# Gates and hidden values of the V product loaded in halves of four experts instead of quarters of two

## The chip, the cores and the metric

The kernel runs on one core of a Trainium2 chip. The metric is the device time in microseconds of one execution; lower is better. The text calls TensorE PE, VectorE DVE, ScalarE ACT, GpSimd POOL and SyncE SP, as the profile does.

## The reference

One layer of a streaming encoder: an input projection, a convolution mixer and a gated linear attention, an output projection, a layer norm, and then a mixer called PEER. The change lies in the last product of PEER. It is this part, cut to what matters:

```python
ids, gates = top 16 of 128 x 128 product keys for each of 8 heads of a token
h = gelu(einsum('td,thkd->thk', xb, u_table[ids]))
w = gates * h
out = einsum('thk,thkd->td', w, v_table[ids])
x = layer_norm(ALPHA * x + out)
```

There are 544 tokens (512 of the prompt, 32 of the sample), 16,384 experts, and rows of 2,048 float32 in u_table and v_table. A token picks 128 experts.

## The kernel before

**Two ways to the same sum.** For 352 tokens (TD) the last product is done densely: a gate matrix g, zero except at the picks, is multiplied by h, and PE multiplies all of V by w = g * h. For the other tokens the picked rows of V are gathered from DRAM by POOL and added on DVE, a slot of 128 rows at a time (192 slots in all; one gather brings 128 rows of 8 KB, 1 MB). Both run at the same time in the stage here called V.

**Stage V.** V is streamed in 128 tiles of 1 MB, in 16 groups of 8 tiles. For each tile:

- SP loads it into `wraw[:, m % 2]` (`v_tile_in`). It may do so once DVE has split the tile that held this half two tiles ago.
- ACT rounds it to float32r in `wh` (L1133), and DVE forms the rest `wl = wraw - wh` (`v_lo_split`, L2040).
- PE runs 48 matmuls of 352 columns: wh with Wh (L1060), wh with Wl (L1061), and last wl with Wh (L1066).
- DVE adds PE's two sums to `acc` (`add_pair`, L2015; L2034 for a single one).

`Wh` and `Wl` hold w of a whole group of 8 x 128 experts, and each exists twice. While PE is in group g, DVE and ACT make those of group g + 1: for each pair q of the 8 expert columns DVE multiplies `wt = hg * gt` (`w_products`, L1993), ACT rounds it to `Wh` (L1475), and DVE forms `Wl` (`w_lows`, L1999). `gt` and `hg` are single buffers of 8 x 352 per partition. `gt` is read from the scratch tensor g_scratch, `hg` from h_scratch, both in DRAM.

**The order on DVE is written out by hand**, as a loop over tiles n = 8g + m. I call such a turn step m of group g. The products of the next group stand in steps 3, 4, 5 and 6, the lows in steps 4, 5, 6 and once more in step 6 behind the first slot. The part of a step that all have is:

```python
add_pair(n)
todo = list(slots_at(n))
for s in todo[:1]:
    slot(s)
...
v_lo_split(n + 2)
for s in todo[1:]:
    slot(s)
```

`slots_at` gives a step one or two slots, 1.66 on average. Steps 0 and 1 have almost nothing to add: three of the 16 output blocks are kept in PSUM to the end (`KEEP`), so step 0 adds nothing and step 1 one block.

**The gathers** have three buffers `gath`. POOL issues `v_gather(s)` when slot s - 3 is done (it waits for `slot_s`), and behind each of them an `h_gather` of 128 single values for a slot eight further on. slot s on DVE waits for its gather.

**The order on SP**: SP issues the tile of its turn (g, m) when DVE has done the split in its step 8g + m - 4, so SP's turn m = 4 follows DVE's step 0, and SP's turn m = 0 follows step 4 of the group before. Behind a tile stands a load for the next group. All of them go through one DMA queue (q1); POOL's gathers go through another (q0). `used(g, q)` makes SP wait until the products that read the old contents are done.

Of the kernel before, what the change touches and what calls it, by code (L numbers as in the profile page):

```python
# [48 lines left out]
EG = 8  # L49
NG = NKEY // EG  # L50
GC = 32
RT, NB = 64, 2
TD = T - P - RT
# [17 lines left out]
def n_op(kind, i):  # L71

    if kind == 4:
        return 7 * i + 8 if i + 1 < NP else 7 * i + 6
    if i == 0:
        return (1, 2, 5, 6, 3, 7).index(kind)
    return 7 * i - 1 + (1, 2, 4, 5, 6, 3, 7).index(kind)
# [75 lines left out]
def program(nc, xT, w_in, w_f, w_out, w_q, u_t, v_t, conv_state, conv_w, conv_vec, gla_state,  # L153
# [3 lines left out]
    with ctx:  # L157
        lo0 = -(-nc.sbuf_base // 32) * 32

        def at(name, shape, dt, off):  # L160
            return nc.alloc_sbuf_tensor_at(name, shape, dt, offset=lo0 + off)

        def sem(name):
            return ctx.enter_context(nc.semaphore(name))
# [72 lines left out]
        o = M1  # L237
# [22 lines left out]
        o = 15520 + 5 * XB + RT * 4  # L260
# [24 lines left out]
        gt = at("gt", [P, EG, TD], F32, S0)  # L285
        hg = at("hg", [P, EG, TD], F32, HG)
# [53 lines left out]
        zero_set, g_zero, g_ids, g_put, pk_s = (  # L340
            sem("zeros_set"), sem("g_cleared"), sem("g_indices"), sem("g_scattered"), sem("rest_packed"))
        h_st = [sem("h_stored0"), sem("h_stored1")]
        g_in = [sem(f"g_pair{q}_in") for q in range(EG // 2)]
        h_in = [sem(f"h_pair{q}_in") for q in range(EG // 2)]

        h_out, w_s, y_add = sem("gelu_out"), sem("w_pair_ready"), sem("y_added")
        xt_s, xt_hi, xt_lo = sem("x_sum"), sem("x_sum_hi"), sem("x_sum_lo")
# [5 lines left out]
        wp_s, wh_s = sem("w_pair_product"), sem("w_pair_hi")  # L353
# [25 lines left out]
        h_dense = h_flat[NKEY * P * SD:].rearrange("(g p n u t) -> g n p u t", g=NG, p=P, u=2, t=TD)  # L379
        h_group = h_flat[NKEY * P * SD:].rearrange("(g p q) -> g p q", g=NG, p=P)  # L380
# [74 lines left out]
        def _(sp):  # L455
            def load(dst, src, s):
                sp.dma_start(dst, src).then_inc(s, 16)
# [62 lines left out]
            for t in range(2 * NP):  # L520
# [7 lines left out]
                g, m = (KU + t) // EG, (KU + t) % EG  # L528
# [1 line left out]
                v_rows_in(g, m)  # L530
            vs = v_t.rearrange("(g n) p k c -> g n p k c", n=EG)

            def g_pair(g, q):
                a = g_rows[g] if isinstance(g, int) else g_rows[bass.ds(g, 1)].rearrange("o j e t -> (o j) e t")
                load(gt[:, 2 * q:2 * q + 2], a[:, 2 * q:2 * q + 2], g_in[q])

            def h_pair(g, q):
                a = h_dense[g, q] if isinstance(g, int) else h_dense[bass.ds(g, 1), q].rearrange("o p u t -> (o p) u t")
                load(hg[:, 2 * q:2 * q + 2], a, h_in[q])

            def v_tile_in(g, m):
                sp.wait_ge(dlo, g * EG + (A_V + m - 1 - D0))
                tile(vs[g, m] if isinstance(g, int) else vs[bass.ds(g, 1), m].rearrange("o p k c -> (o p) k c"), m % 2)

            def used(g, q):
                sp.wait_ge(wp_s, g * (EG // 2) + (q + 1))

            sp.wait_ge(op_lo, n_op(4, NP - 2) + 1)
            tile(vs[0, 0], 0)
            sp.wait_ge(g_put, 16 * PUTS * PH)  # L550
            for q in range(EG // 2):
                g_pair(0, q)
            for v in range(2):
                sp.wait_ge(h_st[v], 32 * (EG // 4))
            sp.wait_ge(prod, n_op(5, NP - 1) + 1)
            for q in range(EG // 2):
                h_pair(0, q)

            def acc_load(j):
                load(acc[:, 4 * j:4 * j + 4], x2_dram[:, 4 * j:4 * j + 4], acc_in[j])  # L560
# [10 lines left out]
            for m in range(2, EG):  # L571
                v_tile_in(0, m)
                if m == 2:
                    for v in range(2):
                        sp.wait_ge(h_st[v], 32 * (NKEY // 4))
                if m < 6:
                    used(0, m - 2)
                    g_pair(1, m - 2)
                    h_pair(1, m - 2)
                else:  # L580
                    used(1, m - 6)
                    g_pair(2, m - 6)

            def v_group_in(g, last=False):

                for m in range(EG):
                    v_tile_in(g, m)
                    if m < 2:
                        used(g, m + 2)
                        g_pair(g + 1, m + 2)  # L590
                    elif m < 6:
                        h_pair(g + 1, m - 2)
                    elif not last:
                        used(g + 1, m - 6)
                        g_pair(g + 2, m - 6)

            with sp.Fori(1, NG - 2) as g:
                v_group_in(g)
            v_group_in(NG - 2, True)
            for m in range(EG):  # L600
                v_tile_in(NG - 1, m)
            for k in range(0, KT, 2):
# [917 lines left out]
        def _(v_):  # L1520
# [28 lines left out]
            def gla(h):  # L1549
# [16 lines left out]
                def distances(l):  # L1566

                    b, n, m = blocks(bcum, l)
                    d, _, _ = blocks(dist[l % 2], l)
                    mid = b[:, :, 0, m - 1:m].to_broadcast([P, n, m])  # L1570
                    tt_(d[:, :, 0], mid, b[:, :, 0], ALU.subtract)
                    C.done(tt_(d[:, :, 1], b[:, :, 1], mid, ALU.subtract), dist_s)
# [410 lines left out]
            def v_lo_first(n):  # L1983
                v_.wait_ge(whi, A_V + n + 1)
                C.inc(tt_(wl[:, n], wraw[:, n], f(wh[:, n]), ALU.subtract), dlo)

            def w_products(g, q):

                e = slice(2 * q, 2 * q + 2)
                v_.wait_ge(g_in[q], g * 16 + 16)  # L1990
                v_.wait_ge(h_in[q], g * 16 + 16)
                v_.wait_ge(w_s, g * (EG // 2) + q)
                C.inc(tt_(wt[:], hg[:, e], gt[:, e], ALU.mult), wp_s)  # L1993

# [66 lines left out]
            def w_lo(e):  # L2061
                v_.wait_ge(wh0_s, e + 1)
                C.inc(tt_(Wl[0][:, e], wt[:, e % 2], f(Wh[0][:, e]), ALU.subtract), w0_s)

            for e in range(EG):
                if e % 2 == 0:
                    v_.wait_ge(g_in[e // 2], 16)
                    v_.wait_ge(h_in[e // 2], 16)
                if e >= 2:
                    v_.wait_ge(w0_s, e - 1)  # L2070
                C.inc(tt_(wt[:, e % 2], hg[:, e], gt[:, e], ALU.mult), wp0_s)
                if e == 1:
                    v_lo_first(0)
                if e:
                    w_lo(e - 1)
# [16 lines left out]
            for n in range((NG - 1) * EG):  # L2092
                g, m = n // EG, n % EG
                if n == (NG - 2) * EG:
                    v_.wait_ge(slot_s, SLOTS)
                    v_.sem_inc(y_sp_s, 1)
                if n > (NG - 2) * EG and m <= 4:
                    v_.wait_ge(y_turn, m)
                    a_ = acc[:, 4 * m - 4:4 * m, T - P:T]
                    C.inc(stt_(a_, a_, ALPHA, ps[:, TURN].rearrange("p (k t) -> p k t", k=4), ALU.mult, ALU.add),  # L2100
                          y_sp_u)
                if 4 <= m < 7:
                    w_lows(g + 1, (g + 1) % 2, m - 4)
                if 3 <= m < 7:
                    w_products(g + 1, m - 3)
# [4 lines that stand above are left out]
                if m == 6:  # L2110
                    w_lows(g + 1, (g + 1) % 2, 3)
# [3 lines that stand above are left out]
# [112 lines left out]
```

## Time and profile before

| | |
|---|---|
| three runs | 3569.99, 3570.5, 3574.88 us |
| median | 3570.5 us |
| the profiled execution's own time | 3572.87 us |
| its span, first to last instruction | 3571.1 us |
| mean granted TensorE clock in it | 0.986 |
| PE, DVE, POOL, ACT busy over the span | 96%, 78%, 55%, 33% |
| DMA moved over the span | 815.58 MB |

The time is that of the whole program; stage V is about its last 1,060 us. The shares of busy time are means over stages with different limits, so the shares above say little of V; the rows below are of V, most of them of the 861 us from 2542.5 to 3403.7, in which 13 whole groups run alike. The profiled execution is 2.4 us above the median.

### The profile page before, as it was taken

Reading aid. Unit: us, or ns where it says so; the run is one execution under the profiler, and the core shown is the slowest. Engines: PE = TensorE matmul, PEld = TensorE weight load, DVE = VectorE, ACT = ScalarE, POOL = GpSimd, SP = SyncE. Lnnn points to the kernel's source line nnn. Section 1 sums busy time; section 2 is a strip of 40 time slices with the busy share of each in tenths; the row PEclk is TensorE's granted clock in tenths of the full one; section 3 lists DMA queues with packets and bytes.
Section 4 is the critical chain, followed back from the end, with each engine's and each line's share of the span. In section 5 each row is a group of like instructions: output and inputs, shape, how many; then the busy total and the mean of one; then the engine's idle time right before and its main releaser. Section 6 shows DMA issues by size and latency. Waiting matters only on the chain. (4 is left out here: it accounts for less than half of the span.)

```text
span 3571.1 us, 62917 instructions
## 1 busy us (share of the span) xinstructions
PE 3442.1 (96%) x25376; PEld 3393.3 (95%) x25376; DVE 2790.6 (78%) x3529; ACT 1187.1 (33%) x1155; POOL 1960.7 (55%) x1165
## 2 busy tenths in 40 slices
PE   8999999998999999999999999999999999999996
PEld 7999999898999999999999999999989999999996
DVE  4866858624799887777777777777898999999997
ACT  2332333323222234444444444443322222222323
POOL 3443434445444577778768850000777778788741
PEclk9999999899999999999999999999999999999998
DMA  4222222473225678888888887777999999999982
GB/s 154 75 77 78 82 73 72 171 285 122 82 91 172 186 207 228 225 228 218 230 224 227 224 224 226 227 228 260 388 369 379 390 366 390 383 374 392 382 320 108
DMA packets 467598, 815.58 MB, mean 228 GB/s; under 512 B 76128, under 2 KB 373632, under 8 KB 399632
## 3 DMA queue, kind: packets, MB, share of 16 engines
q1 hardware_dynamic: 337920, 543.80, 46.3%
q0 software_dynamic: 85184, 201.75, 16.8%
q10 hardware_dynamic: 44368, 68.47, 5.2%
q8 instruction: 64, 1.05, 0.1%
q14 instruction: 62, 0.51, 0.0%
HBM read 740.81 MB, written 207.22 MB: 265 GB/s over the span
## 5 line engine op out<-in xcount | busy, mean ns | idle before, releaser
L618 POOL TENSOR_TENSOR wl<-wraw,wh 128x512 fp32r<-128x512 f32 x352 | 538.6, 1560 | 689.6 <-ACT wh L1133 681.7
L669 POOL DMA_INDIRECT g_scratch<-picks,g_col x384 | 635.7, 1655 | 185.0 <-issue 152.5
L1060 PE MATMUL ps<-Wh,wh 128*128 128x352 f32 x2032 | 660.6, 327 | 49.6 <-DVE Wl L1999 44.6
L1133 ACT ACTIVATE wh<-wraw 128x2048 fp32r<-128x2048 f32 x216 | 413.6, 1915 | 865.0 <-DMA wraw<-in_v_t 478.4
L1061 PE MATMUL ps<-Wl,wh 128*128 128x352 f32 x2032 | 658.1, 326 | 0.0
L1008 PE MATMUL ps<-xh,wl 128*128 128x272 f32 x1792 | 518.8, 290 | 0.0
L1008 PE MATMUL ps<-xl,wh 128*128 128x272 f32 x1792 | 516.0, 288 | 0.0
L1008 PE MATMUL ps<-xh,wh 128*128 128x272 f32 x1792 | 515.8, 288 | 0.3 <-DVE wl L1925 0.3
L710 PE MATMUL ps<-xh,wh 128*128 128x272 f32 x2304 | 491.0, 294 | 17.5 <-DVE ext L1683 11.9
L710 PE MATMUL ps<-xl,wh 128*128 128x272 f32 x2304 | 482.4, 291 | 0.0
L655 POOL DMA_INDIRECT s_h<-h_scratch,s_hid x128 | 245.4, 1917 | 422.2 <-DMA h_scratch<-hb 383.5
L1414 ACT ACTIVATE wh<-wraw 128x1024 fp32r<-128x1024 f32 x280 | 297.1, 1062 | 498.4 <-PE ps L1008 367.4
L1060 PEld LDWEIGHTS ps<-Wh,wh 128*128 128x128 f32 x2032 | 387.1, 191 | 55.5 <-issue 50.6
L710 PEld LDWEIGHTS ps<-xh,wh 128*128 128x128 f32 x2304 | 364.8, 191 | 28.9 <-issue 24.8
L1061 PEld LDWEIGHTS ps<-Wl,wh 128*128 128x128 f32 x2032 | 388.9, 191 | 0.0
L1925 DVE TENSOR_TENSOR wl<-wraw,wh 128x1024 fp32r<-128x1024 f32 x280 | 343.1, 1226 | 47.9 <-ACT wh L1414 39.6
L710 PEld LDWEIGHTS ps<-xl,wh 128*128 128x128 f32 x2304 | 365.2, 190 | 0.0
L1066 PE MATMUL ps<-Wh,wl 128*128 128x352 f32 x2032 | 346.8, 323 | 0.0
L1008 PEld LDWEIGHTS ps<-xh,wh 128*128 128x128 f32 x1792 | 337.6, 188 | 0.5 <-DVE wl L1925 0.5
L1008 PEld LDWEIGHTS ps<-xl,wh 128*128 128x128 f32 x1792 | 337.9, 189 | 0.0
L1008 PEld LDWEIGHTS ps<-xh,wl 128*128 128x128 f32 x1792 | 337.4, 188 | 0.0
L2058 DVE SCALAR_TENSOR_TENSOR y_sp<-gath,s_w,y_sp 128x2048 f32<-128x2048 f32 x127 | 298.5, 2350 | 47.9 <-DMA gath<-v_rows,s_ids 31.9
(319 smaller groups left out, 7039.5 us busy)
## 6 DMA issues: line engine op xcount, KB each, us to landing
wraw<-in_u_t SPq DMA_DIRECT2D x128, 1024.0 KB, 5.2
v_rows<-in_v_t SPq DMA_DIRECT2D x256, 512.0 KB
wraw<-in_v_t SPq DMA_DIRECT2D x128, 1024.0 KB, 8.1
wraw<-in_w_in SPq DMA_DIRECT2D x40, 1024.0 KB, 4.8
g_scratch<-zeros ACTq DMA_DIRECT2D x32, 704.0 KB, 6.4
h_scratch<-hb ACTq DMA_DIRECT2D x64, 352.0 KB, 8.2
gt<-g_scratch SPq DMA_DIRECT2D x64, 352.0 KB, 7.7
hg<-h_scratch SPq DMA_DIRECT2D x64, 352.0 KB, 10.4
```

Of the source, the lines that this page charges most:

```text
L618: ins = nc.gpsimd.tensor_tensor(wl[:, u, part], wraw[:, u, part], f(wh[:, u, part]), ALU.subtract)
L655: nc.gpsimd.indirect_dma_start(column(s_h, x_h, s), None, h_elem, bass.IndirectOffsetOnAxis(ap=column(s_hid, x_hid, s), axis=0)).then_inc( ...
L669: nc.gpsimd.indirect_dma_start(g_elem, bass.IndirectOffsetOnAxis(ap=idx, axis=0), gate, None, compute_op=ALU.add).then_inc(g_put, 16)
L710: ins = mat(out[:, h], w[:, u, k], m[:, k, halves[h]], start=(begin and k == ks[0] and w is wh and m is ah), stop=(end and k == ks[-1] and ...
L1008: ins = mat(bank(kind), w[:, k], m[:, k], start=(k == 0 and w is ah and m is bh), stop=(k == HK - 1 and w is al))
L1060: mat(out, wh[:, u, d * EG + e], Wh[v][:, e], start=(begin and e == 0), stop=False)
L1061: mat(out, wh[:, u, d * EG + e], Wl[v][:, e], start=False, stop=False)
L1066: ins = mat(out, wl[:, u, d * EG + e], Wh[v][:, e], start=False, stop=(end and e == EG - 1))
L1133: go(wh[:, u], wraw[:, u], ACT.Copy).then_inc(whi, 1)
L1414: go(op_part(wh, q), op_src(kind, i), ACT.Copy).then_inc(op_hi, 1)
L1925: C.inc(tt_(op_part(wl, q), op_src(kind, i), f(op_part(wh, q)), ALU.subtract), op_lo)
L2058: C.inc(stt_(y[:], gath[s % 3][:], w, y[:], ALU.mult, ALU.add), slot_s)
```

## The change

The pieces are twice as large and half as many. Before, SP loads a pair of expert columns at a time, 352 KB, one behind each tile: the gates of group g + 1 in SP's turns 6 and 7 of the group before and in turns 0 and 1, and the hidden values in turns 2, 3, 4 and 5. After, it loads four columns at a time, 704 KB: gates behind the tiles of turns 0 and 3, hidden values behind those of turns 2 and 5, and nothing behind those of turns 1, 4, 6 and 7. There are two semaphores for the gates and two for the hidden values where there were four each, and DVE's products wait for the half that holds their pair.

```diff
-            def g_pair(g, q):
+            def g_half(g, j):
+                e = slice(4 * j, 4 * j + 4)
                 a = g_rows[g] if isinstance(g, int) else g_rows[bass.ds(g, 1)].rearrange("o j e t -> (o j) e t")
-                load(gt[:, 2 * q:2 * q + 2], a[:, 2 * q:2 * q + 2], g_in[q])
-
-            def h_pair(g, q):
-                a = h_dense[g, q] if isinstance(g, int) else h_dense[bass.ds(g, 1), q].rearrange("o p u t -> (o p) u t")
-                load(hg[:, 2 * q:2 * q + 2], a, h_in[q])
+                load(gt[:, e], a[:, e], g_in[j])
+
+            def h_half(g, j):
+                e = slice(4 * j, 4 * j + 4)
+                a = h_group[g] if isinstance(g, int) else h_group[bass.ds(g, 1)].rearrange("o p q -> (o p) q")
+                load(hg[:, e], a[:, 4 * j * TD:4 * (j + 1) * TD].rearrange("p (e t) -> p e t", e=4), h_in[j])
...
-            def used(g, q):
-                sp.wait_ge(wp_s, g * (EG // 2) + (q + 1))
+            def used(g, j):
+                sp.wait_ge(wp_s, g * (EG // 2) + 2 * (j + 1))
...
-                if m < 6:
-                    used(0, m - 2)
-                    g_pair(1, m - 2)
-                    h_pair(1, m - 2)
-                else:
-                    used(1, m - 6)
-                    g_pair(2, m - 6)
-
-            def v_group_in(g, last=False):
+                if m in (2, 4):
+                    used(0, m // 2 - 1)
+                    g_half(1, m // 2 - 1)
+                elif m in (3, 5):
+                    h_half(1, m // 2 - 1)
+
+            def v_group_in(g):
 
                 for m in range(EG):
                     v_tile_in(g, m)
-                    if m < 2:
-                        used(g, m + 2)
-                        g_pair(g + 1, m + 2)
-                    elif m < 6:
-                        h_pair(g + 1, m - 2)
-                    elif not last:
-                        used(g + 1, m - 6)
-                        g_pair(g + 2, m - 6)
-
-            with sp.Fori(1, NG - 2) as g:
+                    if m in (0, 3):
+                        used(g, m // 3)
+                        g_half(g + 1, m // 3)
+                    elif m in (2, 5):
+                        h_half(g + 1, m // 3)
+
+            with sp.Fori(1, NG - 1) as g:
                 v_group_in(g)
-            v_group_in(NG - 2, True)
...
-                v_.wait_ge(g_in[q], g * 16 + 16)
-                v_.wait_ge(h_in[q], g * 16 + 16)
+                v_.wait_ge(g_in[q // 2], g * 16 + 16)
+                v_.wait_ge(h_in[q // 2], g * 16 + 16)
```

On SP's queue, the loop over groups begins with the tile of turn 0. `wraw<-in_v_t` is a tile, `gt` the gates, `hg` the hidden values; ISA and REGISTER_ALU rows are SP's waits and address arithmetic. Before:

```order
-L457 DMA wraw<-in_v_t 128x2048
-L546 ISA
-L457 ISA
-L457 DMA gt<-g_scratch 128x704
-L457 ISA
-L457 DMA wraw<-in_v_t 128x2048
-L546 REGISTER_ALU
-L457 ISA
-L457 DMA gt<-g_scratch 128x704
```

And after, at the same place, turns 0, 1 and 2:

```order
+L457 DMA wraw<-in_v_t 128x2048
+L548 ISA
+L457 ISA
+L457 DMA gt<-g_scratch 128x1408
+L457 ISA
+L457 DMA wraw<-in_v_t 128x2048
+L544 REGISTER_ALU
+L457 ISA
+L457 DMA wraw<-in_v_t 128x2048
+L457 ISA
+L457 DMA hg<-h_scratch 128x1408
```

The two pairs behind two tiles have become one half behind the first of them; the first half of the hidden values stands where the first pair of them stood.

Further on in the same loop, SP's turns 3, 4 and 5, which follow DVE's steps 7, 0 and 1. Before:

```order
-L457 DMA wraw<-in_v_t 128x2048
-L457 ISA
-L457 DMA hg<-h_scratch 128x704
-L542 REGISTER_ALU
-L457 ISA
-L457 DMA wraw<-in_v_t 128x2048
-L457 ISA
-L457 DMA hg<-h_scratch 128x704
-L542 REGISTER_ALU
-L457 ISA
-L457 DMA wraw<-in_v_t 128x2048
```

And after:

```order
+L457 DMA wraw<-in_v_t 128x2048
+L548 REGISTER_ALU
+L457 ISA
+L457 DMA gt<-g_scratch 128x1408
+L544 REGISTER_ALU
+L457 ISA
+L457 DMA wraw<-in_v_t 128x2048
+L544 REGISTER_ALU
+L457 ISA
+L457 DMA wraw<-in_v_t 128x2048
+L457 ISA
+L457 DMA hg<-h_scratch 128x1408
```

Behind the tile of turn 3 a half of the gates has moved in, which was spread over later turns before; turn 4 carries nothing, and turn 5 a half.

## Rows read from the trace of the kernel before

**Rows 1.** The page: span, and DMA share in 40 slices

```profile
span 3571.1 us, 62917 instructions
DMA  4222222473225678888888887777999999999982
```

**Rows 2.** What PE waited for, 2542.5 to 3403.7: total us, times, longest

```profile
PE ps L1060 <- DVE Wl L1999: 39.2, 12, 5.3
```

**Rows 3.** What DVE waited for, 2542.5 to 3403.7

```profile
DVE y_sp L2058 <- DMA gath<-v_rows,s_ids: 31.9, 28, 4.1
DVE y_x L2058 <- DMA gath<-v_rows,x_ids: 12.7, 13, 1.8
DVE acc L2015 <- PE ps L1066: 0.6, 1, 0.6
```

**Rows 4.** Windows, from the last low of a group to the next first product

```profile
core 0: us, PE busy (x) PEld busy (x) DVE busy (x) ACT busy (x) POOL busy (x), PEclk, DMA share, GB/s
2676.90:2711.20 34.30, 34.14 (x212) 34.14 (x213) 29.35 (x17) 6.76 (x4) 27.78 (x15) 1.00 0.95 378
...
3140.10:3172.80 32.70, 32.55 (x194) 32.56 (x195) 28.30 (x17) 7.66 (x4) 26.51 (x15) 0.95 0.99 397
...
sum 442.80, PE 441.04 PEld 441.15 DVE 389.82 ACT 100.67 POOL 356.37; mean PE 33.93 PEld 33.93 DVE 29.99 ACT 7.74 POOL 27.41
```

**Rows 5.** Windows, from the first product to the last low of a group

```profile
2643.90:2676.90 33.00, 30.13 (x188) 29.84 (x186) 30.59 (x23) 12.64 (x9) 23.15 (x13) 1.00 0.94 363
...
3303.10:3335.00 31.90, 29.44 (x184) 29.15 (x183) 30.68 (x24) 10.70 (x8) 22.27 (x13) 1.00 0.98 384
...
sum 418.40, PE 372.24 PEld 366.98 DVE 398.51 ACT 137.88 POOL 315.89; mean PE 28.63 PEld 28.23 DVE 30.65 ACT 10.61 POOL 24.30
```

**Rows 6.** SP's queue in order of time, group 5

```profile
2811.24 0.33 SPq L457 DMA_DIRECT2D wraw<-in_v_t  x1
2811.75 0.33 SPq L457 DMA_DIRECT2D hg<-h_scratch  x1
...
2841.34 0.33 SPq L457 DMA_DIRECT2D wraw<-in_v_t  x1
2845.05 0.33 SPq L457 DMA_DIRECT2D gt<-g_scratch  x1
```

**Rows 7.** DVE in order of time, group 5

```profile
2829.63 2.29 DVE L2040 TENSOR_TENSOR wl<-wraw,wh 128x2048 fp32r<-128x2048 f32 x1
...
2836.62 2.35 DVE L2058 SCALAR_TENSOR_TENSOR y_sp<-gath,s_w,y_sp 128x2048 f32<-128x2048 f32 x1 [1.33 <-DMA gath<-v_rows,s_ids]
2838.89 2.29 DVE L2040 TENSOR_TENSOR wl<-wraw,wh 128x2048 fp32r<-128x2048 f32 x1
```

**Rows 8.** ACT in order of time, group 5

```profile
2826.29 1.92 ACT L1133 ACTIVATE wh<-wraw 128x2048 fp32r<-128x2048 f32 x1 [6.01 <-DMA wraw<-in_v_t]
2834.86 1.92 ACT L1133 ACTIVATE wh<-wraw 128x2048 fp32r<-128x2048 f32 x1 [6.65 <-DMA wraw<-in_v_t]
```

**Rows 9.** DMA issues, 2542.5 to 3403.7: count, KB each, median us to landing

```profile
wraw<-in_v_t SPq DMA_DIRECT2D x104, 1024.0 KB, 8.4
hg<-h_scratch SPq DMA_DIRECT2D x52, 352.0 KB, 10.5
gt<-g_scratch SPq DMA_DIRECT2D x52, 352.0 KB, 7.7
```

**Rows 10.** Windows, us 2461 (the first pairs of gates alone) and 8.2 us of group 9

```profile
2461.00:2462.00 1.00, 1.00 (x11) 1.00 (x10) 1.00 (x2) 0.53 (x1) 0.00 (x0) 1.00 1.02 406
3096.60:3104.80 8.20, 8.20 (x53) 8.20 (x53) 5.43 (x4) 3.31 (x2) 5.63 (x5) 1.00 1.02 419
```

**Rows 11.** POOL in order of time, group 5

```profile
2830.84 1.90 POOL L650 DMA_INDIRECT gath<-v_rows,s_ids  x1 [0.30 <-issue]
2833.03 1.96 POOL L655 DMA_INDIRECT s_h<-h_scratch,s_hid  x1 [0.30 <-issue]
2835.30 0.94 POOL L650 DMA_INDIRECT gath<-v_rows,s_ids  x1 [0.30 <-issue]
```

More of the change, by code:

```diff
@@ L342, in program @@
         h_st = [sem("h_stored0"), sem("h_stored1")]
-        g_in = [sem(f"g_pair{q}_in") for q in range(EG // 2)]
-        h_in = [sem(f"h_pair{q}_in") for q in range(EG // 2)]
+        g_in = [sem(f"g_half{j}_in") for j in range(2)]
+        h_in = [sem(f"h_half{j}_in") for j in range(2)]
         h_out, w_s, y_add = sem("gelu_out"), sem("w_pair_ready"), sem("y_added")
@@ L550, in _ @@
             sp.wait_ge(g_put, 16 * PUTS * PH)
-            for q in range(EG // 2):
-                g_pair(0, q)
+            for j in range(2):
+                g_half(0, j)
             for v in range(2):
@@ L555, in _ @@
             sp.wait_ge(prod, n_op(5, NP - 1) + 1)
-            for q in range(EG // 2):
-                h_pair(0, q)
+            for j in range(2):
+                h_half(0, j)
             def acc_load(j):
@@ L2065, in _ @@
             for e in range(EG):
-                if e % 2 == 0:
-                    v_.wait_ge(g_in[e // 2], 16)
-                    v_.wait_ge(h_in[e // 2], 16)
+                if e % 4 == 0:
+                    v_.wait_ge(g_in[e // 4], 16)
+                    v_.wait_ge(h_in[e // 4], 16)
                 if e >= 2:
```

## The prediction

> **What bounds the kernel now.** I read the page first. The share of the DMA engines stands at 9 tenths only in the last quarter of the span [rows 1], and that quarter is stage V, the only place that the change touches. So all that follows is read in V, and there in the 861 us in which 13 groups run alike (66.2 us each).
>
> Next come the waits of PE, since PE has the most work in the program. In V it waits at one place: for DVE's last `Wl` of a group, 39.2 us in 12 times [rows 2]. So PE is held up once a group, for about 3.3 us, and by DVE. Then DVE's own waits: for PE 0.6 us in all, for gathers 31.9 + 12.7 = 44.6 us in 41 times [rows 3]. DVE is therefore the chain that sets V: it never waits for PE, PE waits for it, and what it loses itself it loses to gathers that have not landed. In this stretch a microsecond more or less of DVE's waiting is a microsecond of the kernel.
>
> Where in a group does DVE wait? I cut each group in two, at the last low of a group (step 6) and at the next first product (step 3). The first part, which I call the light stretch, lasts 442.8 / 13 = 34.06 us, and DVE works 29.99 of it [rows 4]: 4.07 us idle. The other part, the heavy stretch with the products and lows of the next group, lasts 418.4 / 13 = 32.18 us with 30.65 us of work [rows 5]: 1.53 us idle, most of that the short gaps at semaphores. So nearly all waiting for gathers is in the light stretch, where DVE has little but slots and splits and asks for them quickly.
>
> The same windows show the DMA engines near full in both: 378 to 397 GB/s in the light ones shown [rows 4], middle about 388; 363 to 384 in the heavy ones [rows 5], middle about 373. The light stretch is where requests come faster than the engines can serve them; in the heavy one there is about 15 GB/s, or 4%, to spare.
>
> **The change, part by part.**
>
> *Fewer instructions on SP.* 64 issues of 0.33 us go [rows 6]. SP waits between tiles anyway: from the issue at 2811.75 to its next gates at 2845.05 it is ahead of its work [rows 6]. Price 0. The waits `used` also go away in effect: the products of both pairs of a half are done before SP's turn comes. That lets the gates start earlier behind their tile (before, the gates at 2845.05 left 3.7 us after their tile at 2841.34 [rows 6]), but nothing stood behind that wait that was ready to go, since the next tile waits for DVE's next split, which comes later than the product. Price 0.
>
> *Lateness of the halves.* The pair landed 7.7 (gates) and 10.5 us (hidden values) after issue [rows 9]; a half carries 352 KB more, 0.36 MB / 388 GB/s = 0.93 us, perhaps twice that when it shares the engines. Its least lead is that of the second hidden half, issued after step 1 and used in step 5, that is, more than three steps of some 8 us. No product waits. In the first group the products run right after older work and the pieces are all issued long before; price 0 to 1 us once, and I take 0.
>
> *Larger pieces as such.* Per group 8 pairs of 0.36 MB are moved, 2.88 MB. When only pairs were in flight they ran at 406 GB/s; the best 8 us with large tiles and gathers gave 419 [rows 10]. If the halves reached that, a group saves 2.88/406 - 2.88/419, or 7.1 - 6.9 = 0.2 us of engine time. Bounds: 0, and 0.6 us if each piece also costs a gap at its start that halving saves. I take 0.2, for 14 groups 3 us, as far as it reaches DVE at all.
>
> *Where the bytes go.* This is the term that decides. SP's turns 2, 3, 4 and 5 come after DVE's steps 6, 7, 0 and 1, so what they issue runs in the light stretch. Before, four pairs stand there, 1.44 MB. After, halves stand behind turns 2, 3 and 5: 2.16 MB. The heavy stretch had four pairs and keeps one half. So 0.72 MB per group move from the stretch with DMA time to spare into the one in which DVE waits for DMA. At 388 GB/s they take 1.86 us. Upper bound: all of it is waited for, 1.86 us per group. Nothing comes back in the heavy stretch, because there DVE's own 30.65 us of work are the length. Lower bound: 0, if the last half, behind turn 5, is in fact still running when the heavy stretch begins and the one in turn 3 is made up for by the empty turn 4. The half behind turn 5 is one of the two that moved in or grew, so I take half of the sum, 0.93 us, less a good 0.1 us of the saving: 0.8 us per group. There are 14 light stretches with the new order (at the start of groups 1 to 14): 14 x 0.8 = 11 us.
>
> *Who shares with whom.* A gather that is under way beside a pair gets the larger part of an engine if the engine takes turns piece by piece: rows of 8 KB against 2.75 KB. Against rows of 5.5 KB it gets less. By bytes the four pieces of 2.75 KB and two of 5.5 KB cost the same; so this adds nothing to the sum over a group, but it points the same way in the light stretch. The Trainium skill ("DMA: Bandwidth & Descriptors", Queues, rings and completion order) says that each DMA engine goes round-robin between the queues that have work, switching at packet boundaries. By that rule a gather beside a half is later than one beside a pair, which speaks against the change; by the byte count alone it would not be. No row here shows the turns themselves.
>
> *Tiles.* A tile issued behind a larger piece lands later, by up to 0.36 MB / 388 = 0.93 us, or 1.86 us when a gather takes every second turn. ACT waits for tiles all the time (6.01 and 6.65 us), and finished at 2828.21 and 2836.78 [rows 8] for splits that DVE began at 2829.63 and 2838.89 [rows 7]: slack of 1.4 and 2.1 us. At the lower lateness this costs nothing; at the upper one 1.86 - 1.4 = 0.4 us per group, 6 us in all. It is in the upper end, not in the sum.
>
> The profiled execution took 3572.87 us, 2.4 above the median of 3570.5. The sum, 3572.9 + 11 = 3584, is therefore 3570.5 + 11 = 3581.5 in medians.
>
> **The rivals.**
>
> *It cancels out (no change).* Three light-stretch pieces and an empty turn may be smoothed by the buffers: three gathers and two tiles. For it: in the light stretch POOL issues without a break, gather, small gather, gather at 2830.84, 2833.03 and 2835.30 [rows 11], 4.46 us per slot, while DVE's late slot began at 2836.62, 3.9 us after the gather of 2830.84 had been issued [rows 7, 11]. If the pace of POOL is what DVE feels, more bytes beside it matter little. Against it: 3.9 us for 1 MB is 270 GB/s, so the landing is shared and not free. The time: 0 to 0.5 us per group, 3564 to 3577, middle 3571.
>
> *Faster.* Four of eight turns carry nothing now, and gathers of steps 0 and 1 may find the engines free at just the right time: turn 4, after step 0, carries nothing, and the slots of step 1 and 2 are gathered then. If each light stretch loses 1 us of its 4.07 us idle, 14 us go: 3556. It decides for this side once the empty turn takes off more than the halves at turns 2, 3 and 5 add, that is, if the empty turn is worth more than 1.86 us. The end of it is all of the gather waits, 44.6 us in 13 groups. For it speaks that the waits fall on steps 0 to 2, on both sides of turn 4; against it, that turn 4 loses 0.36 MB and its neighbours gain 0.36 MB each. The Trainium skill (the same page, Rules for kernel authors) asks for at least 1 MiB per DMA and for small transfers to be joined, and gives about 2 us as the fixed part of one; by that, four loads fewer a group would be up to 8 us of engine time, an estimate from that page. The 406 GB/s of pairs that run one behind the other [rows 10] do not show such a gap, so in this kernel the fixed part overlaps.
>
> *Slower than forecast.* All 1.86 us are waited for and the tiles come late as well: 14 x (1.86 + 0.4) = 32 us, 3602.
>
> **How the numbers follow.** A difference under 0.2% (7 us) cannot be told from none here: the three runs lie 5 us apart. Forecast, slower by 7 to 27 us (3578 to 3597): 0.45. Beyond it: 0.05. Cancels: 0.28. Faster: 0.22. So faster 0.22, same 0.28, slower 0.50. The forecast's own range is 3578 to 3597. For 8 in 10 I go down to 3558, which leaves about half of the faster case out, and up to 3599.
>
> **What the profile after would show.** DVE's waits for gathers in the like stretch at 55 to 60 us where they were 44.6; PE's waits for `Wl` at some 50; the light stretches 0.8 us longer, the heavy ones as they were; in the light ones the same GB/s, in the heavy ones less. DVE's busy time, PE's, and the bytes the same. No product waits for `gt` or `hg`. It would be wrong if the light stretches keep their length with more bytes in them (their GB/s up to 405 or so: then the engines had room there), if a DVE split waits for ACT (tiles late), or if gathers land sooner beside fewer, larger pieces.

## The result, and the profile after

The kernel became slower, by 0.45%: ratio 1.0045, 95% interval 1.0033 to 1.0057, median 3589.74 us of five runs where before has 3571.66 us of five. The forecast was 11 us; it is 18 us by medians, 16 us by the ratio.

The profiled execution of the changed kernel took 3588.32 us. Its page, to be held against [rows 1]:

```profile
span 3586.5 us, 62756 instructions
DMA  4222222463225678889888887778999999999982
DMA packets 458382, 815.58 MB, mean 227 GB/s; under 512 B 75104, under 2 KB 372608, under 8 KB 390416
```

The bytes are the same to the last digit shown (815.58 MB). The span is 15.4 us longer.

The waits of PE and DVE, in the 13 like groups (2544.5 to 3417.6 us; lines 4 lower than before), answer to [rows 2, 3]. `DVEq` is DVE's sequencer, and `issue` is time in which the engine waited for nothing that the trace shows. First PE:

```profile
PE ps L1056 <- DVE Wl L1995: 42.9, 12, 5.2
PE ps L1056 <- DVEq L2012: 4.9, 4, 1.7
PE ps L1056 <- issue: 2.1, 1, 2.1
```

And DVE:

```profile
DVE y_sp L2054 <- DMA gath<-v_rows,s_ids: 41.7, 34, 3.9
DVE y_x L2054 <- DMA gath<-v_rows,x_ids: 15.3, 14, 2.9
...
DVE wl L2036 <- ACT wh L1129: 1.4, 1, 1.4
```

DVE waits 41.7 + 15.3 = 57.0 us for gathers where it waited 44.6 us [rows 3], and in 48 places where there were 41. No product waits for `gt` or `hg`; no such row is among the waits. One split waits for ACT, 1.4 us in all. PE's three rows make 49.9 us where the same rows made 43.2 us. For the row of `Wl` some 50 us had been expected, and it is 42.9. PE's busy time did not stay the same either: its 4,992 matmuls took 820.0 us where they took 813.3, at a mean granted clock of 0.983 over the program where it was 0.986. DVE waits for PE nowhere in these groups, so this is not what lengthened them.

The light stretches (last low of a group to the next first product), two of the 13 and the sum, to be held against [rows 4]:

```profile
3283.10:3317.30 34.20, 34.03 (x203) 34.04 (x204) 29.42 (x17) 8.40 (x5) 24.03 (x15) 0.95 0.99 392
3349.20:3385.40 36.20, 36.06 (x225) 36.07 (x226) 31.79 (x19) 9.60 (x5) 28.34 (x16) 1.00 0.98 388
sum 454.60, PE 452.89 PEld 453.00 DVE 390.45 ACT 115.81 POOL 351.56; mean PE 34.84 PEld 34.85 DVE 30.04 ACT 8.91 POOL 27.04
```

And the heavy ones, against [rows 5]:

```profile
3317.30:3349.20 31.90, 29.15 (x183) 28.82 (x181) 30.67 (x24) 9.88 (x8) 22.27 (x13) 1.00 0.96 372
3385.40:3417.60 32.20, 25.92 (x161) 25.34 (x159) 30.62 (x24) 8.93 (x7) 26.03 (x13) 0.98 0.92 358
sum 418.50, PE 367.06 PEld 360.92 DVE 398.19 ACT 123.96 POOL 315.14; mean PE 28.24 PEld 27.76 DVE 30.63 ACT 9.54 POOL 24.24
```

The light stretch grew from 442.8 / 13 = 34.06 to 454.6 / 13 = 34.97 us, with the same work in it (390.45 us where there were 389.82). The heavy ones stayed to a tenth of a microsecond in sum: 418.5 and 418.4. So 11.8 of the 15.4 us lie in 13 light stretches. The rest lies at the ends. The first like group starts at 2544.5 where it was 2542.5 (+2.0), and 1.0 us of that lies ahead of stage V, which the change does not touch:

```profile
2455.63 0.33 SPq L457 DMA_DIRECT2D wraw<-in_v_t  x1
2456.64 0.33 SPq L457 DMA_DIRECT2D wraw<-in_v_t  x1
```

This is the first tile of V, before and after. The stretch of group 14 behind the 13, from the last low to the next, took 71.6 us where it took 68.9 (+2.7). Its light part, which is the 14th light stretch, took 37.8 us where it took 36.5 (+1.3). What follows took 1.3 us less.

### The profile page after: what moved, and what is told of

Same layout as the page of the kernel before. It is cut to its first block and busy times, and to the rows that moved or that the text cites. A ratio compares the mean times of both kernels' runs of the same rounds, so it can differ in the third digit from the quotient of the medians.

```text
span 3586.5 us, 62756 instructions
## 1 busy us (share of the span) xinstructions
PE 3448.6 (96%) x25376; PEld 3399.6 (95%) x25376; DVE 2791.4 (78%) x3529; ACT 1188.5 (33%) x1155; POOL 1956.6 (55%) x1165
## 2 busy tenths in 40 slices
DMA packets 458382, 815.58 MB, mean 227 GB/s; under 512 B 75104, under 2 KB 372608, under 8 KB 390416
## 3 DMA queue, kind: packets, MB, share of 16 engines
q0 software_dynamic: 85184, 201.75, 16.9%
## 5 line engine op out<-in xcount | busy, mean ns | idle before, releaser
L706 PE MATMUL ps<-xh,wh 128*128 128x272 f32 x2304 | 490.8, 294 | 17.4 <-DVE ext L1679 11.9
L2054 DVE SCALAR_TENSOR_TENSOR y_sp<-gath,s_w,y_sp 128x2048 f32<-128x2048 f32 x127 | 298.7, 2352 | 55.8 <-DMA gath<-v_rows,s_ids 41.7
```

Source lines behind the costliest of these rows:

```text
L706: ins = mat(out[:, h], w[:, u, k], m[:, k, halves[h]], start=(begin and k == ks[0] and w is wh and m is ah), stop=(end and k == ks[-1] and ...
L2054: C.inc(stt_(y[:], gath[s % 3][:], w, y[:], ALU.mult, ALU.add), slot_s)
```

## The experiments

All are compared with the kernel before on the same chip. Two words recur. **Place**: behind which tile a load stands. **Size**: how much one load carries. The first four vary one or the other. Where a diff starts with `...`, the loads of the first group are left out of it; they were moved in the same way.

**Pairs at the places of the halves.**

```diff
...
-                    if m < 2:
-                        used(g, m + 2)
-                        g_pair(g + 1, m + 2)
-                    elif m < 6:
-                        h_pair(g + 1, m - 2)
-                    elif not last:
-                        used(g + 1, m - 6)
-                        g_pair(g + 2, m - 6)
+                    if m in (0, 3):
+                        for q in (2 * (m // 3), 2 * (m // 3) + 1):
+                            used(g, q)
+                            g_pair(g + 1, q)
+                    elif m in (2, 5):
+                        for q in (2 * (m // 3), 2 * (m // 3) + 1):
+                            h_pair(g + 1, q)
```

> Pairs of 352 KB as before, but two of them behind each tile that carries a half in the changed kernel (turns 0, 2, 3, 5): only the places are changed, not the size. Theory P (place: 0.72 MB per group moved into the light stretch sets the loss): as slow as the changed kernel, 12 to 20 us over before. Theory S (size: a gather beside a 5.5 KB row gets less of an engine, or long pieces hold tiles up): within 5 us of before.

Measured: ratio 1.0029 (1.0019 to 1.0039), 3584.3 us. The place alone, at the old size, costs 10 us. The windows of its trace give light stretches of 35.0 us and heavy ones of 32.1, like the changed kernel's. How DVE loses the time is not quite the same: it waits 49.9 us for gathers from 2540 to 3420 (before 46.4, changed 58.4), and the rest is spread over short waits, of splits for ACT (3.0 us) and for PE among others.

**Halves at even places.** The edit is against the changed kernel: the first half of the gates goes from turn 0 to turn 7, the second from turn 3 to turn 1.

```diff
...
-                    if m in (0, 3):
-                        used(g, m // 3)
-                        g_half(g + 1, m // 3)
+                    if m == 1:
+                        used(g, 1)
+                        g_half(g + 1, 1)
                     elif m in (2, 5):
                         h_half(g + 1, m // 3)
+                    elif m == 7 and not last:
+                        used(g + 1, 0)
+                        g_half(g + 2, 0)
```

> Halves of 704 KB, gates behind turns 7 and 1, hidden values behind turns 2 and 5: light stretch 1.44 MB as before, only the size is changed. Theory P: within 5 us of before, light stretches 34.0 to 34.3 us. Theory S: 10 to 20 us over before.

Measured: 1.0018 (1.0010 to 1.0027), 3579.1 us, 6 to 7 us over before, with light stretches of 34.5 us in its trace. The second half of the gates has gone from the light stretch, and with it 10 us of the changed kernel's loss (1.0045 to 1.0018). But not all: with the light stretch's 1.44 MB restored, 6 us remain. Neither theory alone had it.

**All eight pairs in the light stretch.**

```diff
...
-                    if m < 2:
-                        used(g, m + 2)
-                        g_pair(g + 1, m + 2)
-                    elif m < 6:
-                        h_pair(g + 1, m - 2)
-                    elif not last:
-                        used(g + 1, m - 6)
-                        g_pair(g + 2, m - 6)
+                    if 2 <= m < 6:
+                        used(g, m - 2)
+                        g_pair(g + 1, m - 2)
+                        h_pair(g + 1, m - 2)
```

> Pairs of 352 KB, all eight of a group behind turns 2 to 5: 2.88 MB in the light stretch where before has 1.44. Theory P by the measured size (0.9 us per 0.72 MB and group): 2 x 0.9 x 14 = 25 us over before, up to 50 if all is waited for. Theory S: within 8 us of before, since the size is that of before.

Measured: 1.0087 (1.0072 to 1.0103), 3602.9 us, 31 us over before. Twice the shift, at the old size, gives three times the 10 us that the single one gave. What is new at this dose is a second kind of wait, in DVE's waits from 2540 to 3420 us:

```profile
DVE y_sp L2051 <- DMA gath<-v_rows,s_ids: 35.2, 26, 4.7
DVE y_x L2051 <- DMA gath<-v_rows,x_ids: 17.0, 13, 4.7
DVE wl L2033 <- ACT wh L1126: 16.9, 13, 2.9
```

and in PE's:

```profile
PE ps L1053 <- DVE Wl L1992: 39.9, 12, 4.6
PE ps L1053 <- ACT wh L1126: 16.0, 13, 2.5
```

Now tiles come too late as well: a split waits once a group for ACT, 16.9 us in 13 times, and ACT waits for the tile. Before, no split waited in these groups. With it the heavy stretch grows too, from 32.18 to 33.32 us, while the light one is at 35.23: about half of the loss lies in each.

**Most pairs in the heavy stretch.** The other direction: gates and hidden values of one pair together behind turns 7, 0, 1 and 2, so that the light stretch holds 0.72 MB.

```diff
...
+                    if m < 3:
+                        used(g, m + 1)
+                        g_pair(g + 1, m + 1)
+                        h_pair(g + 1, m + 1)
+                    elif m == 7 and not last:
+                        used(g + 1, 0)
+                        g_pair(g + 2, 0)
+                        h_pair(g + 2, 0)
```

> Pairs of 352 KB, gates and hidden values of a pair behind turns 7, 0, 1 and 2: 0.72 MB in the light stretch where before has 1.44. Theory P: 0.9 us per group less, 10 to 15 us faster than before. Theory S, or if the light stretch is set by the pace of POOL: within 5 us of before.

Measured: 1.0012 (1.0003 to 1.0021), 3576.6 us. Not faster; if anything slower. The place theory, read as a scale that works in both directions, misses: adding 0.72 MB to the light stretch costs 10 us, taking 0.72 MB from it gives nothing. Its waits for gathers in the same 880 us, 29.8 + 15.6 + 1.6 = 47.0 us, are those of before (31.9 + 13.2 + 1.3 = 46.4 us), and its light stretches are not shorter (34.36 us). The result lies in the other bracket, that of size or of POOL's pace.

**Two pairs behind one tile, at even places.** The places of the second experiment with the size of before; the diff is that of the second with `for q in` two pairs in place of one half.

> Pairs of 352 KB, two of them behind each of the turns 7, 1 (gates) and 2, 5 (hidden values): the places of the kernel with halves at even places, with the size of before. If that kernel lost its 7 us by the size of its rows: this one stands within 3 us of before. If it lost them by bunching (two pairs behind one tile and none behind the next): 7 us over before, like it.

Measured: 1.0002 (0.9993 to 1.0011), 3574.5 us: no change. So bunching two pairs behind a tile costs nothing, and the 6 us of halves at even places belong to the halves. Beside the first experiment this is also the cleanest test of the place: the same pairs, two by two, with the gates behind turns 0 and 3 there (1.0029) and behind turns 7 and 1 here (1.0002).

**Eighths.**

```diff
-                load(gt[:, 2 * q:2 * q + 2], a[:, 2 * q:2 * q + 2], g_in[q])
+                for e in (2 * q, 2 * q + 1):
+                    load(gt[:, e], a[:, e], g_in[q])
...
-                load(hg[:, 2 * q:2 * q + 2], a, h_in[q])
+                for u in range(2):
+                    load(hg[:, 2 * q + u], a[:, u], h_in[q])
```

> Each pair is loaded as two single columns of 176 KB, one behind the other, at the places of before: only the size of rows and loads is changed, to the half. Theory S (a gather gets less of an engine beside longer rows, 6 us lost by doubling them): 3 to 8 us faster than before. If smaller pieces cost engine time (fixed cost of a load, the view behind joining transfers): 3 to 15 us slower. If size does nothing: within 3 us.

Measured: 0.9995 (0.9987 to 1.0004), 3571.4 us: no change. 256 loads of half the size in place of 128 gave nothing and cost nothing.

**Without the loads of groups 2 to 15.** The calls in the loop are taken out, and the products from group 2 on no longer wait for them.

> Leaves out the loads of gates and hidden values for groups 2 to 15; the products use those of group 1. It prices all of this traffic. If the loads' bytes are what the gathers wait for in the light stretch, its gather waits fall from 3.7 us per group to under 1 and the kernel gains 35 to 50 us. If the pace of POOL sets the waits, they stay over 2.5 us and the gain is under 15 us.

Measured: 0.9959 (0.9945 to 0.9974), 3560.0 us: 12 to 15 us faster, for 14 x 2.88 = 40 MB less. The profiled execution is the slowest of its four (3566.07 us), 7 us under the one of before. DVE's waits, from 2540 to 3420 us:

```profile
DVE y_sp L2048 <- DMA gath<-v_rows,s_ids: 25.2, 21, 4.3
DVE y_x L2048 <- DMA gath<-v_rows,x_ids: 10.9, 9, 3.8
...
DVE acc L2005 <- PE ps L1055: 7.7, 4, 2.6
...
DVE acc L2024 <- PE ps L1055: 4.4, 7, 1.6
```

The waits for gathers fell by 10 us only, to 25.2 + 10.9 + 0.4 = 36.5 us; the 0.4 us is a row left out. And a new wait has come, for PE: 12.1 us in 11 times where there was 0.6 us. By the bracket set beforehand (a gain under 15 us, waits over 2.5 us per group) this is the case in which the loads' bytes are not what mainly sets the waits. They are one part of it.

**Without the small gathers.** POOL's `h_gather` from the ninth on is left out, and the slots from the eighth on take the values of the first eight.

> Leaves out the gathers of 128 single values that POOL issues between its gathers of rows (slots from the eighth on use the values of the first eight); about 1% of the bytes, nearly half of POOL's work. If the pace of POOL sets the gather waits, they fall from 3.7 us per group to under 1 and the kernel gains 30 to 50 us. If the engines' load sets them, they stay over 2.5 us and the gain is under 15 us.

Measured: 0.9972 (0.9963 to 0.9981), 3562.8 us: 10 us faster. Gather waits in its 13 like groups are 21.7 + 11.3 + 1.7 = 34.7 us, 2.7 per group, where they were 45.9, 3.5 per group. This is the bracket in which POOL's pace does not mainly set the waits (gain under 15 us, waits over 2.5). So of the two last runs each took one suspect away, and each gave only the small gain: both are a part of the wait, and neither is the whole.

**One load of 704 KB with short rows.** The halves at even places once more, with 16 bytes of padding behind each pair in `gt` and `hg`, so that a row of 5.5 KB falls into two of 2.75 KB. The diff is against the changed kernel, cut to the loads of the gates.

```diff
-        gt = at("gt", [P, EG, TD], F32, S0)
+        gq = at("gt", [P, EG // 2, 2 * TD + 4], F32, S0)
+        gt = gq[:, :, 0:2 * TD].rearrange("p q (u t) -> p q u t", u=2)
...
-                load(gt[:, e], a[:, e], g_in[j])
+                load(gq[:, 2 * j:2 * j + 2, 0:2 * TD], a[:, e].rearrange("p (q u) t -> p q (u t)", u=2), g_in[j])
```

> The kernel with halves at even places, but gt and hg have 16 bytes of padding behind each pair, so that the 704 KB of a half go as rows of 2.75 KB in place of 5.5 KB, in one load. If the 6 us that halves cost against two pairs at the same places come from the length of the rows: they go, within 3 us of before. If they come from the load being one of 704 KB: they stay, 5 to 9 us over before.

Measured: 1.0019 (1.0010 to 1.0029), 3579.2 us, the same as with long rows (1.0018). By the times, the length of the rows is not what the halves cost. The trace cannot confirm it: its execution is the fastest of the 11 (3571.32 us, median 3579.15), and its light stretches, 33.98 us, are as short as with pairs.

**Eighths at the places of the halves.**

> Single columns of 176 KB, four behind each turn that carries a half in the changed kernel: the crowded places with the shortest rows. If shorter rows leave gathers more of the engines, it lies below the 12 us over before that pairs gave at these places: 5 to 9 us over. If the size matters only above some length, like the pairs: 10 to 14 us over.

Measured: 1.0047 (1.0033 to 1.0061), 3590.0 us. Neither bracket: it is as slow as the changed kernel, with rows a quarter as long. Pairs at these places gave 1.0029. In the times there is no order by size here: 176, 352 and 704 KB give 1.0047, 1.0029 and 1.0045. But the eighths lose their time in another way. DVE's waits, 2540 to 3420 us:

```profile
DVE y_sp L2056 <- DMA gath<-v_rows,s_ids: 26.0, 24, 2.8
DVE y_x L2056 <- DMA gath<-v_rows,x_ids: 12.3, 11, 2.7
DVE wl L2038 <- ACT wh L1131: 10.9, 9, 2.6
...
DVE y_x L2053 <- DMA gath<-v_rows,x_ids: 2.8, 1, 2.8
```

The waits for gathers, 41.1 us, are below those of before (46.4 us). In their place splits wait for ACT, 10.9 us in 9 times: the tiles are late. DVE waits another 4.3 us for PE.

**Without loads and without small gathers.**

> Leaves out both the loads of gates and hidden values for groups 2 to 15 and the small gathers after the first eight. If a floor lies close under the kernel (PE, held up at the group's border, is late for DVE's steps 1 and 2), the two gains of 12 and 10 us do not add up: 12 to 17 us under before, and DVE waits for PE 15 us or more in V. If gathers alone set the light stretch: 22 to 40 us under before.

Measured: 0.9938 (0.9923 to 0.9953), 3548.9 us: 22 to 25 us faster, where the two alone gave about 15 and 10 by their ratios. They add up, as in the bracket for gathers alone. DVE's waits, 2540 to 3420 us:

```profile
DVE y_sp L2047 <- DMA gath<-v_rows,s_ids: 19.4, 20, 2.4
DVE y_x L2047 <- DMA gath<-v_rows,x_ids: 10.3, 9, 2.6
...
DVE acc L2003 <- PE ps L1053: 8.9, 6, 2.4
...
DVE acc L2022 <- PE ps L1053: 3.2, 5, 1.1
```

12.1 us of waits for PE, no more than with the loads alone gone. So PE takes back a part of the gain, but there is no hard floor close under the kernel.

**The last low ahead of the slot.**

```diff
                 add_pair(n)
+                if m == 6:
+                    w_lows(g + 1, (g + 1) % 2, 3)
                 todo = list(slots_at(n))
                 for s in todo[:1]:
                     slot(s)
-                if m == 6:
-                    w_lows(g + 1, (g + 1) % 2, 3)
```

> Eighths at the places of before, and on DVE the last low of a group stands ahead of the slot of step 6 and not behind it. PE then starts a group up to 2.35 us earlier. If the floor is PE's late start, this gives 5 to 15 us; if DVE's own work and gathers are all that counts, within 3 us of before.

Measured: 1.0018 (1.0009 to 1.0027), 3578.4 us, slower than the eighths that it starts from (0.9995). PE's waits, 2540 to 3420 us:

```profile
PE ps L1062 <- DVE Wl L2001: 22.7, 13, 3.1
PE ps L1062 <- DVEq L2018: 20.7, 18, 1.7
PE ps L1062 <- ACT wh L1135: 4.0, 6, 1.3
```

The wait for the last low fell to 22.7 us from 44.6 us in the same stretch of before, and as much came back at other places, behind DVE's additions. Neither bracket had a slower kernel. DVE's waits for gathers rose as well, to 33.6 + 15.5 + 1.2 = 50.3 us from 40.7 us with the eighths that it starts from. PE's start is not what sets the time. No version that does all the work beat the kernel before clearly.

**The traces side by side.** V is the time from its first tile to the end of the program; light and heavy are means of 13 stretches; the last column is what DVE waited for gathers from 2540 to 3420. Each row is one execution.

| loads | ratio of the times | V, us | light, heavy, us | gathers, us |
|---|---|---|---|---|
| places of before, pairs (the kernel before) | 1 | 1115.5 | 34.06, 32.18 | 46.4 |
| places of before, eighths | 0.9995 | 1116.6 | 34.08, 31.99 | 40.7 |
| even places, pairs two by two | 1.0002 | 1121.2 | 34.03, 32.28 | 44.2 |
| even places, halves | 1.0018 | 1125.8 | 34.50, 32.29 | 49.3 |
| even places, halves with short rows | 1.0019 | 1118.7 | 33.98, 32.27 | 44.0 |
| mostly heavy, pairs | 1.0012 | 1120.0 | 34.36, 32.09 | 47.0 |
| halves' places, eighths | 1.0047 | 1132.8 | 35.35, 31.89 | 41.1 |
| halves' places, pairs | 1.0029 | 1129.5 | 34.98, 32.07 | 49.9 |
| halves' places, halves (the changed kernel) | 1.0045 | 1129.9 | 34.97, 32.19 | 58.4 |

Two things stand out. All three kernels with the halves' places have light stretches of 35 us, and none of the others in the table has. And at the same places the waits for gathers are the longer, the longer the rows of the loads beside them, while the kernel's time does not follow. Single executions are to be read with care: V's first tile lies anywhere from 2447.2 to 2456.6 us in them, though all the edits lie behind it. On a few microseconds the ratios decide, from 5 to 12 runs each.

## Why the prediction was right

- **DVE, not PE, sets V, and it loses its time in the light stretch**: shown. The whole growth per group is there, with DVE's work unchanged, DVE waits for PE nowhere in the changed kernel's like groups, and the earlier start for PE gave nothing.
- **Bytes moved into the light stretch, 0.8 us per group**: it measured 34.97 - 34.06 = 0.91 us. That the place costs time is shown: pairs at the halves' places cost 10 us against before and against the same pairs at even places, halves taken back to even places lose 10 of the 16 us, and the double dose costs 31 us. That it is the count of bytes in the stretch, as a scale, is not shown: half of the bytes taken out of it gave nothing. The rates fit the choice of "half of the sum", but do not prove it: with 0.72 MB more issued in it, the light stretch carried only 0.25 MB more of all kinds, since the mean rates over the 13 windows give 34.06 us x 388 GB/s = 13.2 MB before and 34.97 x 385 = 13.5 MB after. The rest, of loads or of gathers, ran later. The slack in the heavy stretch was real: its length did not change, at 365 GB/s where it had 373.
- **14 groups, 11 us**: mis-sized. The 14 light stretches gave 11.8 + 1.3 = 13.1 us and not 11. Another 1.4 us in the heavy stretch of group 14 and 1.0 us in group 0 had no term, 1.0 us lies ahead of V, and 1.3 us came back at the end. In all 15.4 us in the profiled pair. The forecast came out close in part by luck: the half was a choice between two bounds that no row fixed, and by the ratios the place cost 10 us where 14 x 0.93 = 13 had been put, while the size added 6 us where it had been put at a saving of about 2.
- **Larger pieces save 0.2 us per group**: not seen, and of the other sign where it could be measured. One load of 704 KB cost 6 us against two of 352 KB behind the same tiles (1.0018 and 1.0002). The upper bound of 0.6 us for a gap at each piece's start rests on no run, and twice as many loads at the places of before cost nothing (0.9995). Nor do they show the up to 8 us of engine time a group that the rival "faster" took from the Trainium skill's fixed part of a DMA. That estimate misread its page: "DMA: Bandwidth & Descriptors", Anatomy of one DMA, fits the 2 us to DMAs issued from GpSimd and puts them down mainly to completion latency. By the times, the padded version speaks against the row length. One difference between these two is left besides the size: with halves, the gates wait in `used` for the second product of their half, so the first pair's bytes leave one product later. SP's queue shows it, the halves first, then the pairs:

```profile
2656.13 0.33 SPq L457 DMA_DIRECT2D gt<-g_scratch  x1
2661.67 7.71 SPq L457 DMA_DIRECT2D wraw<-in_v_t  x2
2673.17 0.33 SPq L457 DMA_DIRECT2D gt<-g_scratch  x1
```

```profile
2650.61 5.16 SPq L457 DMA_DIRECT2D gt<-g_scratch  x2
2661.01 7.72 SPq L457 DMA_DIRECT2D wraw<-in_v_t  x2
2669.03 3.79 SPq L457 DMA_DIRECT2D gt<-g_scratch  x2
```

  The halves leave at 2656.13 and 2673.17; of the pairs the first leave at 2650.61 and 2669.03, 5.5 and 4.1 us earlier. Of this 1.2 and 0.7 us are there already at the tile ahead, which left at 2651.14 and 2669.05 with halves, and at 2649.99 and 2668.40 with pairs. Whether this lateness or the size of the load costs the 6 us was not separated. The changed kernel does not wait there; SP's only row of waits in it is for splits. At its own places halves and pairs, 1.0045 and 1.0029, lie apart by the same 0.0016, which is about the width of their intervals, while in the profiled executions V is equally long with both (1129.9 and 1129.5 us). How much of its loss is size stays open: between nothing by the traces and a third by the ratios.
- **A gather gets less of an engine beside longer rows** (the view with the Trainium skill's rule of turns between queues, "DMA: Bandwidth & Descriptors", Queues, rings and completion order): the kernel's time does not support it. Rows of 2.75 KB in one load cost what rows of 5.5 KB did, and rows of 1.4 KB were no better, at the places of before (0.9995) or at crowded ones (1.0047). The waits for gathers do go that way: 40.7 and 46.4 us beside rows of 1.4 and 2.75 KB at the places of before, 44.2 and 44.0 beside 2.75 KB and 49.3 beside 5.5 KB at even places, 41.1, 49.9 and 58.4 us at the halves' places. So the view may be right about the gathers and still be worth no time here, since other waits of DVE came in their place, for late tiles with the eighths at the halves' places (10.9 us). These are single executions, and no trace shows the turns themselves.
- **Tiles late, in the upper end**: 1.4 us once in the changed kernel. It becomes a second channel when the light stretch carries more (16.9 us of split waits with all eight pairs in it), and with eighths at the halves' places (10.9 us).
- **"A microsecond more or less of DVE's waiting is a microsecond of the kernel"**: it held for more and not for less. In the changed kernel 12.4 us more of gather waits went with 11.9 us more in the 13 groups. With the loads gone, gather waits fell by 10 us and 12 us of waits for PE appeared; with 0.72 MB less in the light stretch the gather waits did not fall at all. The rival "faster" rested on that sentence.
- **The rival of POOL's pace**: it is a part. Half of POOL's work gone is worth 10 us, all the loads gone 12 to 15 us, both 22 to 25 us, and 30 us of gather waits are still there. The prediction's row against this rival was misread. The slot at 2836.62 did not wait for the gather issued at 2830.84: there are three buffers, gather and slot go in order, and counted back from the gather that POOL issued when a slot was done, it waited for this one:

```profile
2827.29 0.95 POOL L650 DMA_INDIRECT gath<-v_rows,s_ids  x1 [0.30 <-issue]
```

  Its issue ended 8.4 us before the slot began, not 3.9, so 1 MB came at 125 GB/s and not 270. That makes the landing more shared, not less. With a landing of 8 us and three buffers, the number of buffers may be what holds the 30 us; no run changed it.

## What to carry to other kernels

Where several engines are full in turns, ask in which stretch of the loop a transfer runs, not only how large it is: in this kernel the same bytes cost 10 us more when gates moved into the stretch in which the bounding engine waits for DMA. Such a balance can be lopsided: adding to the tight stretch cost at once, while taking as much out of it gave nothing, and taking all the loads away gave 12 to 15 us, partly eaten by waits for the next engine. Look at what a loss consists of, too: a light stretch of 35 us was lost to gathers in one kernel and in part to late tiles in another. Joining loads also joins their waits, so a large one leaves as late as its last part allows.

## What was not expected of the hardware

Below 352 KB the number of loads did not matter at the places of before: 256 loads of 176 KB, in rows of 1.4 KB, in place of 128 of 352 KB, gave 0.9995 (0.9987 to 1.0004). At the halves' places the eighths (1.0047) were slower than pairs (1.0029). And taking away all of this traffic, with the DMA engines' mean rate in V falling from 381 to 340 GB/s, gave only 0.4%: a share near 1 of the DMA engines did not mean that they were the one bound.
